# A hybrid layer in fp32: the preparation moved into the first group's steps, and another order for two W_out tiles

## The reference, cut to what matters

```
u = RMSNorm_pre(x)
p = u @ W_in                  # split in x, g (RG-LRU) and q, k, v, o, i, f (mLSTM)
xc = conv4(p_x); r, i = sigmoid(blockdiag(xc)); h = scan(a, sqrt(1-a^2)*i*xc)
y_rg = RMSNorm(h * gelu(p_g))
log_i = p_i + b_i; log_f = log_sigmoid(p_f + b_f)      # 4 + 4 columns, one per head
y_ml = headRMSNorm(sigmoid(o) * mLSTM(silu(conv4 q), silu(conv4 k), v, log_i, log_f))
x = x + RMSNorm_post(concat(y_rg, y_ml) @ W_out)
x = x + RMSNorm_post(relu(RMSNorm_pre(x) @ W_up)^2 @ W_down)
```

## Time and profile before

| what | us |
|---|---|
| median of three runs | 2466.69 |
| the profiled execution's own time | 2467.44 |
| its span in the trace | 2465.6 |
| first matmul of the mixers | 141.85 |
| first matmul of the output stage | 835.09 |
| first matmul of the second half of the output stage, after a wait | 1652.39 |
| PE busy | 2335.1 (95% of the span) |
| DVE, ACT, POOL busy | 1278.3, 642.5, 834.4 |

### The profile page before, as it was taken

The page is one execution under the profiler, slowest core; times in us unless marked ns, Lnnn a source line. Parts: engine busy times, 40 slices in busy tenths (PEclk is TensorE's granted clock), DMA queues, the critical chain, the costliest instruction groups (busy, mean ns, idle before and its releaser), DMA issues.

```text
span 2465.6 us, 29981 instructions
## 1 busy us (share of the span) xinstructions
PE 2335.1 (95%) x10696; PEld 1943.9 (79%) x10696; DVE 1278.3 (52%) x1584; ACT 642.5 (26%) x1159; POOL 834.4 (34%) x486
## 2 busy tenths in 40 slices
PE   5779999999999599999999999979899999999998
PEld 5758888888887487888888888868688888888886
DVE  5345665656656256445435444517755434534535
ACT  3315554545545232001101101114201101100112
POOL 8400000000000108536435534610746534633630
PEclk9689999999999799999999999989899999999999
DMA  4634453635542552112111101327412111101203
GB/s 171 245 119 153 149 190 121 218 122 174 165 165 71 170 163 94 43 52 68 34 43 60 51 34 51 102 98 244 144 51 69 43 42 51 60 27 50 68 17 145
DMA packets 125177, 254.85 MB, mean 103 GB/s; under 512 B 8105, under 2 KB 43137, under 8 KB 125121
## 3 DMA queue, kind: packets, MB, share of 16 engines
q1 hardware_dynamic: 97008, 157.37, 19.0%
q0 software_dynamic: 24320, 88.35, 11.4%
q10 hardware_dynamic: 3792, 8.47, 0.9%
HBM read 201.67 MB, written 50.40 MB: 102 GB/s over the span
## 4 chain that ended last, share of the span: by engine, by line
PE 60%; DVE 3%; issue 1%; ACT 1%; DMA 1%; POOL 0%; ACTq 0%; DVEq 0%; SPq 0%; PEldq 0%; POOLq 0%
PE o_ps L1350 20%; PE o_ps L1352 20%; PE o_ps L1351 20%; DVE o_relu L1626 1%; DVE o_ff_lo L1630 1%; ACT o_ps L1451 1%; PE o_ps L1374 0%; DMA o_v_lo<-ylo_d 0%; DVE o_acc L1570 0%; DVE o_v_lo L1619 0%; DMA o_w_raw<-in_w_out 0%; DVE o_h_t L1586 0%; ACT o_ff_hi L1508 0%; DVE o_h_t L1599 0%; DVE o_v_t L1607 0%
## 5 line engine op out<-in xcount | busy, mean ns | idle before, releaser
L1319 POOL TENSOR_TENSOR w_hi<-o_w_raw,one 128x1024 fp32r<-128x1024 f32 x100 | 191.7, 1917 | 685.2 <-PE o_ps L1352 594.7
L1350 PE MATMUL o_ps<-o_v_hi,w_hi 128*128 128x512 f32 x1024 | 400.1, 391 | 4.8 <-DVE o_v_lo L1619 4.8
L1351 PE MATMUL o_ps<-o_v_lo,w_hi 128*128 128x512 f32 x1024 | 399.6, 390 | 0.0
L1352 PE MATMUL o_ps<-o_v_hi,w_lo 128*128 128x512 f32 x1024 | 399.6, 390 | 0.0
L1640 DVE TENSOR_TENSOR o_acc<-o_ps,o_acc 128x512 f32<-128x512 f32 x224 | 154.2, 690 | 377.5 <-PE o_ps L1352 377.2
L658 PE MATMUL m_unit_ps<-u_hi,w_hi 128*128 128x512 f32 x768 | 309.4, 403 | 6.3 <-issue 6.3
L1626 DVE TENSOR_TENSOR o_relu<-o_relu 128x512 f32<-128x512 f32 x128 | 218.8, 1710 | 182.7 <-ACT o_relu L1505 181.7
L1505 ACT ACTIVATE o_relu<-o_ps 128x512 f32<-128x512 f32 x128 | 76.5, 597 | 874.9 <-PE o_ps L1352 843.3
L658 PE MATMUL m_unit_ps<-u_hi,w_lo 128*128 128x512 f32 x768 | 301.5, 393 | 0.0
L658 PE MATMUL m_unit_ps<-u_lo,w_hi 128*128 128x512 f32 x768 | 299.9, 390 | 0.0
L1630 DVE TENSOR_TENSOR o_ff_lo<-o_relu,o_ff_hi 128x512 fp32r<-128x512 f32 x128 | 243.1, 1899 | 90.8 <-ACT o_ff_hi L1508 90.8
(11 more groups left out here) (255 smaller groups left out, 3639.5 us busy)
## 6 DMA issues: line engine op xcount, KB each, us to landing
o_w_raw<-in_mlp_w_up POOLq DMA_DIRECT2D x64, 512.0 KB, 4.7
o_w_raw<-in_mlp_w_down POOLq DMA_DIRECT2D x64, 512.0 KB, 3.6
u_hi<-uhi_d SPq DMA_DIRECT2D x14, 2048.0 KB, 10.6
u_lo<-ulo_d SPq DMA_DIRECT2D x14, 2048.0 KB, 15.0
w_raw<-in_w_in POOLq DMA_DIRECT2D x24, 512.0 KB, 4.8
p_xu<-in_x SPq DMA_DIRECT2D x16, 512.0 KB, 7.9
uhi_d<-u_hi SPq DMA_DIRECT2D x4, 2048.0 KB, 7.5
ulo_d<-u_lo SPq DMA_DIRECT2D x4, 2048.0 KB, 13.1
```

The costliest lines, as they stand in the source:

```text
L1319: pool.tensor_tensor(w_hi[i], w_raw[i % 2][:], one_bc, ALU.mult).then_inc(w_split[i], 1)
L1350: nc.tensor.matmul(dst, sh, mh, start=(i == 0), stop=False)
L1351: nc.tensor.matmul(dst, sh, ml, start=False, stop=False)
L1352: last = nc.tensor.matmul(dst, sl, mh, start=False, stop=(i == n - 1))
```

## The change

The preparation block and its clearing of semaphores are gone. The mixers' block begins with the first four tiles of x only: squares, 1/rms, eight groups of transposes (L505), high part (L620) straight from PSUM with the gain as scale, low part straight from PSUM too (`low_of_x`). Then period 0 starts. Periods 0 to 3 each begin with `gate_unit`, 24 matmuls for the eight gate rows of their own tile (L515). Periods 0 to 2 also prepare the tile of the next period: squares ahead of take q, root and scaling behind the exponentials, transposes in the gaps behind slots 3, 4 and 5. Periods 0 to 3 make the gate rows of their tile on 16 partitions, in three parts among VectorE's other work (`chunk_locals`, `chunk_maxima`, `chunk_rows`), with two small trips through DRAM. The gates' weights come from DRAM in four DMAs a period where one came from SBUF. In all periods VectorE's `decay_arguments` moves from the period's head to behind the q convolution. In the output stage the parts of the first two tiles are projected in another order, and the last two W_out tiles are split by ScalarE and VectorE in place of GpSimd.

```diff
-            build_prepare(nc, a, k)
-            clear_semaphores(nc, k)
@@ SP in the mixers @@
+            def store_u(t):
+                sp.wait_ge(ulo_made, KT * (t + 1))
+                for dst, src in ((k["uhi_d"], u_hi), (k["ulo_d"], u_lo)):
+                    sp.dma_start(dst[:, :, t * TILE:(t + 1) * TILE], src[:, t % 2].bitcast(F32)).then_inc(u_out[t % 2], 16)
             def load_rows(p):
...
-                sp.dma_start(gate_w[:], k["gate_w"][:, ds(p // NT, 1), :, :]).then_inc(gate_w_in, 16)
+                if isinstance(p, int) and p < NT:
+                    sp.wait_ge(const_made, 8)
+                    sp.wait_ge(rows_made, p + 1)
+                    for n, row in enumerate((e1_row, e2_row)):
...
+                    sp.wait_ge(rows_out, 32 * (p + 1))
+                for r, name in enumerate(("rg_gate_r_w", "rg_gate_i_w")):
+                    for h in range(2):
+                        sp.dma_start(gate_w[64 * h:64 * h + 64, r, 64 * h:64 * h + 64],
...
-            with sp.Fori(0, STEPS // 2 - 1) as j:
+            store_u(0)
+            load_rows(0)
+            store_u(1)
+            load_rows(1)
+            store_u(2)
+            store(0)
+            load_rows(2)
+            store_u(3)
+            load_u(4, 0)
+            store(1)
+            load_rows(3)
+            load_u(5, 1)
+            store(2)
+            load_rows(4)
+            store(3)
+            with sp.Fori(2, STEPS // 2 - 1) as j:
@@ TensorE @@
             def gates_and_transposes(m):
...
+                if isinstance(m, int) and m < NT - 1:
+                    pe.wait_ge(if_copied, m + 2)
...
+            for p in range(NT):
+                gate_unit(p)
+                for n, u in enumerate(UNITS):
+                    unit(u, p, p % 2)
+                    if p:
+                        slots[n](p - 1)
+                    chain(p, n)
+                    if p < NT - 1:
+                        for c in gap_tiles.get(n, ()):      # {3: (0, 1, 2), 4: (3, 4, 5), 5: (6, 7)}
+                            transpose_x(p + 1, c)
@@ ScalarE, period @@
                 if mix:
                     sigmoids_1(m)
+                if gates:
+                    copy_gates(p)
+                if prepare:
+                    squares(p + 1)
                 if project:
                     take("q")
...
                 if mix:
                     exponentials(m, g_m)
+                if gates:
+                    gate_exponential(p)
+                if isinstance(p, int) and 0 < p <= NT:
+                    floor_columns(p - 1)
+                if prepare:
+                    root_x(p + 1)
@@ VectorE, period @@
                 if mix:
-                    decay_arguments(m)
...
                     convolve("q", p, g_p)
                 if mix:
+                    decay_arguments(m)
...
+                if gates:
+                    gate_absolute(p)
+                if prepare:
+                    inverse_rms(p + 1)
...
                     states(m)
+                if gates:
+                    chunk_locals(p)
...
+                low_parts_x(3)
                 if project:
                     convolve("x", p, g_p)
                     keep_history(p)
+                if gates:
+                    chunk_maxima(p)
...
+                low_parts_x(4)
                 low_of("x")
                 if mix:
                     rg_square_sums(m)
                     rg_low(m)
+                if gates:
+                    chunk_rows(p)
+                low_parts_x(5)
@@ output stage @@
+                    if rnd == "out" and i >= SLOTS - 2:
+                        pool.wait_ge(w_split[i], r * 2 + 2)
+                        continue
...
-                for i in range(2):
-                    project(B, i, i, 0)
-                    project(B, i, i, 1)
+                for part in range(2):
+                    for i in range(2):
+                        project(B, i, i, part)
...
+                for i in (SLOTS - 2, SLOTS - 1):
+                    dve.wait_ge(w_split[i], B * (NF + 1) * 2 + 1)
+                    nc.vector.tensor_tensor(w_lo[i], w_raw[i % 2][:], w_hi[i].bitcast(F32), ALU.subtract
```

More of the change, by code:

```diff
@@ L510, in build_mixers @@
         gate_w = sb("gate_w", [P, 2, P])
+        hist = sb("hist", [P, 3, 3])
+        with ExitStack() as first:
+            x_first = [first.enter_context(nc.sbuf_tensor(f"m_x_first{i}", [P, D], F32)) for i in range(CPT)]
         xbuf = sb("xbuf", [P, 3, TILE + 3])
-        hist = sb("hist", [P, 3, 3])
         conv = {u: sb("conv_" + u, [P, TILE]) for u in "qkx"}
@@ new lines, in _ @@
+            one_bc = k["one"][:].unsqueeze(2).broadcast_to([P, KT, P])
+            for c, u in enumerate(UNITS):
+                pool.wait_ge(raw_first[c % 3], 16 * (c // 3 + 1))
+                pool.tensor_tensor(w_hi[u][:], w_raw[c % 3][:], one_bc, ALU.mult).then_inc(w_split[u], 1)
+                pool.wait_ge(w_split[u], 1)
+                pool.tensor_tensor(w_lo[u][:], w_raw[c % 3][:], w_hi[u][:].bitcast(F32), ALU.subtract
+                                   ).then_inc(w_split[u], 1)
+                if c < 3:
+                    pool.wait_ge(w_split[u], 2)
+                    load_first(c + 3)
@@ L627, in _ @@
+            for t in range(NT - 1):
+                load_x(t + 1)
+                gate_rows(t)
+            pool.wait_ge(x_tr, KT * NT)
             for c in range(3):
                 load_raw(c, 1)
+            gate_rows(NT - 1)
             with pool.Fori(1, NG - 1) as g:
@@ L682, in gates_and_transposes @@
                 pe.wait_ge(s["k_silu"], s.ready(m))
+                if isinstance(m, int) and m < NT:
+                    pe.wait_ge(rows_made, m + 1)
                 for c in range(CPT):
@@ new lines, in gate_unit @@
+            def gate_unit(p):
+                pe.wait_ge(ulo_made, KT * (p + 1))
+                if p:
+                    pe.wait_ge(prev_made, p)
+                for c in range(KT):
+                    for z, (w, x) in enumerate(((wif_hi, u_hi), (wif_hi, u_lo), (wif_lo, u_hi))):
+                        last = nc.tensor.matmul(n_ps[0:2 * NG, :], w[:, c, :], x[:, p % 2, c, :],
+                                                start=(c == 0 and z == 0), stop=(c == KT - 1 and z == 2))
+                last.then_inc(if_mm, 1)
@@ L737, in _ @@
+            for p in (NT, NT + 1):
+                for n, u in enumerate(UNITS):
+                    unit(u, p, p % 2, 32)
+                    slots[n](p - 1)
+                    if p == NT:
+                        chain(p, n)
+            with pe.Fori(0, (STEPS - NT) // 2 - 1) as j:
+                for b in range(2):
+                    p = j * 2 + (NT + 2 + b)
                     for n, u in enumerate(UNITS):
-                        unit(u, p, b)
+                        unit(u, p, b, j * 32 + 64)
@@ L739, in _ @@
                         slots[n](p - 1)
-            for n, u in enumerate(UNITS):
-                unit(u, STEPS - 1, 1)
-                slots[n](STEPS - 2)
             for slot in slots:
```

683 lines of the change are left out of this document (307 added, 376 removed), and 9 rows, old and new, of the table base.

## The result

The changed kernel took 2489.3 us in the median of four runs (2486.6 to 2496.1), the kernel before 2467.0: a ratio of 1.0092, 95% interval 1.0080 to 1.0105. Run again with the last experiments it took 2495.4 (2494.2 to 2496.8), a ratio of 1.0113 (1.0096 to 1.0129) to the kernel before, which took 2466.7 beside it. So it is about 1% slower, where 2481 (+0.6%) was forecast. The profiled execution has a span of 2486.7, 21.1 more than before; the forecast had 13.8.

A forecast was written before the change was run, and what follows sets the result against it. The prediction took the mixers to be bound by TensorE. To the profiled 2467.4 us it added +7.4 for the mixers, -1 for decay_arguments, +2.8 and +4.6 for the output stage: +13.8, 2481 us, range 2440 to 2500.

The forecast's parts named there:

- The sign: Whole kernel: slower, 2481 us against the profiled 2467.4, +13.8; chance of slower 0.63.
- the three stalls: Mixer periods 2, 3, 4: late y or gate weights hold up TensorE, costing 9.8, 21.9 and 8.6 us.
- both halves of the output stage: Output stage: the new projection order makes TensorE and VectorE wait, +2.8 us in the first half, +4.6 in the second.
- period 5 to the output stage (decay_arguments): Drain behind the last period: VectorE reaches head_low 1.4 us earlier, so 1 us gained; nothing in steady periods.
- The start and period 1: Beginning of mixers: gate_unit at 27.5, period 1 at 79.5, 98 us ahead of before; period 1 lasts 60.4.
- The stores of y: SP's queue, periods 2 to 4: y lands behind u at +19.4, +31.5, +26.5, delaying ScalarE's square of g_x.
- Rival A: Periods 2 to 4: y is not held behind u, 40 us of the sum go, 2441 us; chance 0.23.
- The landing at +6: Periods 2 to 4: if y lands by +6 us of its period, ScalarE's square never decides.
- the 13.9 taken from the earlier trace: SP's queue in the old preparation: a load issued behind a 4 MB store of u reached ScalarE 13.9 us later.
- a cold start: TensorE: 3 us added wherever it has been idle for over 5 us.
- B: Periods 0 to 3: VectorE's small steps and gate rows' DRAM trips cost 5 us more each, 2501; chance 0.12.
- C: Output stage: the 12.84 us wait goes and the adds do not slip, 2463 us; chance 0.08.

The follow-up runs named there:

- experiment 1: Changed kernel with SP issuing the stores of y ahead of the stores and loads of u in periods 2, 3, 4: 2443.5 us, ratio 0.9908.
- experiment 12: The changed kernel run and profiled once more, nothing altered: 2495.4 us; the output stage began at 857.7 us.
- Experiment 6: The kernel before with only the new order of the first four projections, GpSimd's split as before: 2474.8 us.
- experiment 7: The kernel before with only the split of W_out tiles 6 and 7 moved to ScalarE and VectorE: 2467.0 us.
- experiments 5: Changed kernel, SP's first-group order altered: gate weights before the wait for rows, y between the rows' two trips, u behind both: 2435.3 us.
- experiment 10: Changed kernel with y-first SP order, old projection order, and VectorE's last two low parts of x ahead of rg_low and chunk_rows: 2411.4 us.

## Why the prediction was right, and where its sizes were off

The sign, the three stalls and both halves of the output stage came out as forecast. Set against the first profile:

| step | forecast | measured |
|---|---|---|
| gate_unit(0) | 27.5 | 29.2 |
| period 1 begins | 79.5 | 79.6 |
| period 1 lasts | 60.4 | 59.0 |
| y lands in period 2, period lasts | +19.4, 73.2 | +23.9, 75.0 |
| y in period 3, period | +31.5, 77.3 | +34.7, 80.7 |
| y in period 4, period | +26.5, 58.0 | +29.4, 61.5 |
| period 5 begins | 348.4 | 355.8 |
| period 5 to the output stage (decay_arguments) | -1 | -1.9 |
| output, first half | +2.8 | +3.6 |
| output, second half | +4.6 | +5.1, of which 0.5 comes back |
| sum | +13.8 | +21.1 |

**The start and period 1** were right within 2 us each; that period 1 begins within 0.1 us of the forecast is two errors that cancel, since gate_unit was 1.7 later (TensorE waited 3.89 for the low part of the gates' weights, `m_wif_lo`, which the forecast did not have) and period 0 shorter. The idle time was forecast for slot 4 and the end of the period, and stands there: 2.4 and 5.2.

**The stores of y** are the step on which the sign was said to rest, and experiment 1 shows it: O is 44 us earlier without most of the stalls (by a measure that varies by 8 to 10 from one execution to the next, experiment 12), the forecast gave them 40. Rival A, with y not held, was put at 2441, and the kernel with y ahead of u takes 2443.5; so the rival's price was right and its condition false. The landing at +6 at which the prediction had this decided is wrong too: in experiment 1 y lands at +12.7 and slot 0 waits 0.17 us. Two terms were mis-sized. One is when SP comes to y: the forecast let SP pass the rows at +4, and it passed them at +7.3 in period 2, since the rows' way to DRAM took 4.7 us from the second store to the first gate load and was counted too short. That is 3.3 of the 4.5 us by which y was late there; the rest is the other term, the landing, 15.3 us behind the issue against the 13.9 taken from the earlier trace rows. In period 3, 3.2 us late, SP passed the rows at +5.6 and the landing took 17.3. In period 4, 2.9 us late, it is the landing alone: y was issued at +11.6, where the forecast's +26.5 less 13.9 gives +12.6, and took 17.8, behind a load of 4 MB and not a store. The three periods are 1.8, 3.4 and 3.5 longer than forecast; less the 1.4 by which period 1 was shorter, that is the 7.4 us by which period 5 came later. Of the two halves of the rule of the Trainium skill (DMA: Bandwidth & Descriptors, Queues, rings and completion order) that the prediction weighed, the first (an issuer's descriptors are taken in ring order) is the one that decided here: by the trace's times from issue to landing, the low half of y landed 1.3 us behind the last of u in each of the three periods. The second half showed once and gave nothing: in period 4 the high half landed 1.6 us ahead of `u_lo`, but the square waits for both.

**What was not in the sum** is that the clock can fall behind waits far shorter than the 5 us of idling at which the forecast took a cold start. Behind 2.2 and 2.4 us it held in some executions and fell in others; slot 0 of period 5 is at +15.0 against before in the first profile (361.3 against 346.3) and at +24.4 in the second (370.7). The profile of before has no such wait in its first group, so this could not be read there, but it belonged in the range. With it the loss is 22 us in one set of runs and 29 in the other, against a forecast of 14: that the first number is the nearer one is luck.

**Output stage.** Experiment 6 (order alone, +7.1 against the 7.7 expected) and 7 (split alone, nothing that the times can tell) confirm the working: the order costs, by the waits of 1.30 and 1.51 us in the first half and the late add of tile 8 in the second. That the faster split is worth nothing because y sets the start of the first half is in the rows (`o_v_lo<-ylo_d`); that the loads behind GpSimd's splits of tiles 4 and 5 set the second is argued, not tested. `scale_rg` ends the wait at 1668.46 and part 0 of tile 9 starts 0.15 later. The forecast had this start 0.7 us ahead of the one in before; it was 0.3 ahead (1652.39 + 12.9 + 3.6 = 1668.9).

**Rivals.** B (longer chains) was not the case: period 1 is 1.4 shorter than forecast. But experiments 5 and 10 show that VectorE's order at the end of a period was worth 11 to 16 us once the stalls were gone. C is refuted by experiment 7.

## What to carry to other kernels

A stage that runs beside others brings its transfers into their queues. Before merging two stages, list for each small store on which an engine waits the bytes that will be under way in front of it; here 256 KB took 15.3 us to land behind 4 MB and 6.3 ahead of them, and putting it first turned a kernel 0.9% slower than before into one 0.9% faster. Moving the large transfer to another queue helped far less than letting the small one go first: 15 us of 46, and those where the small one also went ahead of a load. And work that an engine does for the next stage goes ahead of work whose result nobody awaits yet: two instructions moved forward by 3.5 us in each of two periods were worth 11 to 16, since the clock held as well. The best version, experiment 10, takes 2411.4: 2.2% below the kernel before.

## What the runs showed of the hardware

- The granted TensorE clock can fall behind a wait of 2.2 to 2.4 us or hold (the same instruction took 1.02 and 1.67, the same gate unit 5.56 and 7.13), and with it O moves by 9.7 us from one profile to the next. The fall can come after work has begun again: the first rows behind a wait of 2.24 took 0.39, those from 1.4 us on 0.63. Behind 1.78 us it held in all three waits of experiment 10, behind 5.24 the rows were slow at once in every profile. The length of the wait alone does not decide: ahead of gate_unit of period 0 the clock held behind 3.89 (first profile of the changed kernel) and was low behind 2.77 (experiment 1).
- With 4 to 8 MB just issued in the same queue, the next issue by SP of a 256 KB store took 5.6 to 8.1 us, where it takes 0.34 to 0.5 in a steady period; SP itself is held, and with it all that it would issue next.
- 4 MB in another queue lengthened the issue of four small loads and the rows from 3.0 to 6.0 us, and the landing of the 256 KB from 6.3 to 8.4.
